# A chain of two transformer models: expert weights loaded in runs of 4 KB, two transfers a unit

## The reference

```
order = jnp.argsort(flat_e)                       # token-expert pairs sorted by expert
...
xs = x_pad[row_tok].reshape(n_blocks, MOE_BLOCK, D)          # blocks of 128 rows
def expert_block(args):
    xb, e = args
    return (jax.nn.silu(xb @ w_gate[e]) * (xb @ w_up[e])) @ w_down[e]
...
out = jnp.zeros((N + 1, D), ys.dtype).at[row_tok].add(ys)[:N]
```

## Time and profile before

| | us |
|---|---|
| median of 3 runs | 3743.65 (3742.29 to 3743.70) |
| span of the profiled execution, first to last instruction | 3737.3 |
| PE busy in it | 3342.8 (89%) |
| DVE busy | 1622.3 (43%) |
| transfers of queue q1 (hardware, which SP issues on) | 737.20 MB, 49.5% of 16 engines' time |

### The profile page before, as it was taken

How to read it: one execution, slowest core, us unless ns; L and a number is a source line. 1 busy time by engine, 2 the same in 40 slices (tenths; PEclk the granted TensorE clock), 3 DMA queues, 4 the chain that set the end, 5 groups by cost and what they waited for, 6 DMA issues and landing times. The chain is left out here.

```text
span 3737.3 us, 51196 instructions
## 1 busy us (share of the span) xinstructions
PE 3342.8 (89%) x20706; PEld 1722.0 (46%) x20706; DVE 1622.3 (43%) x2561; ACT 816.9 (22%) x1811; POOL 364.5 (10%) x355
## 2 busy tenths in 40 slices
PE   7999899699999698999995999995999968886996
PEld 3444565333333244777753333332555658443332
DVE  3660886511011574777755011113333874453114
ACT  0000660100000122555501000001333542010112
POOL 1000300210000000000001100000000900003110
PEclk9999999799999899999997999998999979887998
DMA  9990211599999622000024999997213200419996
GB/s 382 353 319 1 91 69 68 228 405 427 424 423 423 233 79 78 4 1 1 1 102 181 401 426 425 427 422 290 97 69 112 102 1 4 172 67 347 417 419 269
DMA packets 146708, 818.39 MB, mean 219 GB/s; under 512 B 29891, under 2 KB 35651, under 8 KB 100390
## 3 DMA queue, kind: packets, MB, share of 16 engines
q1 hardware_dynamic: 117494, 737.20, 49.5%
q0 software_dynamic: 25808, 68.88, 4.8%
q10 hardware_dynamic: 3168, 8.96, 0.6%
HBM read 752.52 MB, written 82.55 MB: 223 GB/s over the span
## 5 line engine op out<-in xcount | busy, mean ns | idle before, releaser
L2272 PE MATMUL m_yp<-m_w,m_hidT 128*32 128x512 f32 (+2 forms) x2248 | 377.2, 594 | 9.2 <-DVE m_yt L2025 3.8
L2249 PE MATMUL m_up<-m_w,m_xT 128*32 128x512 f32 (+2 forms) x1792 | 304.7, 606 | 21.1 <-DMA m_w<-in_moe_w_up 21.1
L2249 PE MATMUL m_gp<-m_w,m_xT 128*32 128x512 f32 (+2 forms) x1792 | 304.9, 600 | 9.4 <-DMA m_w<-in_moe_w_gate 5.9
L2030 DVE TENSOR_TENSOR m_hid<-m_sg,m_up 128x512 f32<-128x512 f32 x42 | 28.9, 687 | 578.4 <-PE m_up L2249 578.4
L2025 DVE TENSOR_TENSOR m_yt<-m_yp,keep_flat 128x512 f32<-128x512 f32 x128 | 82.4, 686 | 392.9 <-PE m_yp L2272 388.9
L412 PE MATMUL front_acc<-front_hT,front_wt 128*128 128x512 f32 x512 | 224.2, 599 | 7.2 <-DMA front_wt<-in_na_w_qkv 7.2
L2272 PEld LDWEIGHTS m_yp<-m_w,m_hidT 128*32 128x32 f32 (+2 forms) x2248 | 121.1, 123 | 217.0 <-issue 211.6
L2249 PEld LDWEIGHTS m_up<-m_w,m_xT 128*32 128x32 f32 (+2 forms) x1792 | 104.0, 126 | 216.1 <-issue 216.1
L2327 ACT ACTIVATE m_sg<-m_gp 128x512 f32<-128x512 f32 (+1 forms) x64 | 33.5, 524 | 772.9 <-PE m_gp L2249 543.7
L2249 PEld LDWEIGHTS m_gp<-m_w,m_xT 128*32 128x32 f32 (+2 forms) x1792 | 99.5, 125 | 209.0 <-issue 207.3
L1191 PE MATMUL n_acc<-n_wt,n_hT 128*128 128x512 f32 (+2 forms) x512 | 191.0, 529 | 2.5 <-DMA n_wt<-in_w_in 1.8
(11 more groups left out here) (493 smaller groups left out, 4936.3 us busy)
## 6 DMA issues: line engine op xcount, KB each, us to landing
m_w<-in_moe_w_gate SPq DMA_DIRECT2D x64, 2048.0 KB
m_w<-in_moe_w_up SPq DMA_DIRECT2D x64, 2048.0 KB
m_w<-in_moe_w_down SPq DMA_DIRECT2D x64, 2048.0 KB
v<-in_ada_w SPq DMA_DIRECT2D x40, 1024.0 KB, 12.7
m_w<-in_moe_w_gate SPq DMA_DIRECT2D x32, 1024.0 KB
m_w<-in_moe_w_up SPq DMA_DIRECT2D x32, 1024.0 KB
m_w<-in_moe_w_down SPq DMA_DIRECT2D x32, 1024.0 KB, 26.5
v<-in_w_mod SPq DMA_DIRECT2D x24, 1024.0 KB, 11.5
```

Source lines behind the costliest of these rows:

```text
L2249: last = pe.matmul(acc[part, 0:F], xT[:, j, k, part], w[:, place_of[m_, r][0], k * F:(k + 1) * F], start=k == 0, stop=k == KC - 1)
L2272: last = pe.matmul(yp[e][part, :], hidT[:, k, part], w[:, place_of["d", r][0], k * D + e * 512:k * D + (e + 1) * 512], start=k == 0, stop= ...
```

## The change

Each unit's one transfer becomes two. The new function `strips` views the partition's 16 KB (8 KB) as runs of 1024 numbers, 4 KB, and takes every second one: the first transfer has the runs 0 and 2, the second the runs 1 and 3 (in the third mixture run 0 and run 1). Slot and memory are viewed alike, so the data land where they did. No two runs of one transfer touch. Both transfers add 16 to the slot's semaphore, and PE waits for 32 a use. The loads of the spill loop stay as they are.

```diff
@@ -1895,6 +1895,10 @@
         def cols(e):
             return slice(e * 512, (e + 1) * 512)
 
+        def strips(v, odd):
+
+            return v.rearrange("p (a b n) -> p b a n", b=2, n=D)[:, odd]
+
         at = {}
         with st.block() as block:
 
@@ -2074,7 +2078,8 @@
                     expert = sp.value_load(pl[0:1, r:r + 1], min_val=0, max_val=LAYERS_EXPERTS - 1)
                     if before is not None:
                         sp.wait_ge(done[before[0]], before[1] + 1)
-                    sp.dma_start(w[:, slot], sources[m_][ds(expert, 1)].rearrange("a p n -> (a p) n")).then_inc(w_in[slot], 16)
+                    for odd in range(2):
+                        sp.dma_start(strips(w[:, slot], odd), strips(sources[m_][ds(expert, 1)].rearrange("a p n -> (a p) n"), odd)).then_inc(w_in[slot], 16)
 
                 for unit in layout.units[:AHEAD]:
                     load(*unit)
@@ -2224,7 +2229,7 @@
                 def arrived(m_, n):
                     for r, _, _ in layout.blocks[n][1]:
                         slot, use = place_of[m_, r]
-                        pe.wait_ge(w_in[slot], 16 * use)
+                        pe.wait_ge(w_in[slot], 32 * use)
 
                 def gate_up(n):
                     j = n % 2
```

## The result

The changed kernel takes 3805.55 us (median, 3802.5 to 3807.63) against 3743.68 us (3742.29 to 3746.32) for the kernel before in runs on the same chip: a ratio of 1.0163, 95% interval 1.0151 to 1.0175. It is slower, as forecast, but by 62 us and not by 25: above the range's upper end of 3793. The profiled execution spans 3800.4 us, 63.1 more than before.

A forecast was written before the change was run, and what follows sets the result against it. The weight transfers on full DMA engines were taken to bound mixtures 1 and 2, with the third nearly tied. 11.5 + 11.5 + 2.5 = 25.5 us on the span of 3737.3 gives 3762.8, plus 6.35 makes 3769; range 3750 to 3793.

The forecast's parts named there:

- The mixtures are bound by their transfers, and nothing else moves: Three mixtures: DMA share 1.01 mid-stage; transfers set the length of 1 and 2, nearly tie in 3; between them nothing moves.
- the engines are full from the first load: Mixtures 1 and 2: engines full from the first load (700) to the last, so all added transfer time lies on the path.
- Runs of 4 KB cost 0.12 us a unit more: Mixtures 1 and 2: 4 KB runs pass slower than 16 KB; 96 x 0.12 = 11.5 us a mixture (0 to 32).
- Mixture 3: +2.5: Third mixture: 4 KB in place of 8 KB runs costs 3.6 us over 96 units, the first covered, so 2.5.
- the cover that I had forecast: Third mixture's end: a unit lands at 3657.6, PE begins its block at 3658.68, so about 1 us of cover.
- A fixed tail: End of mixtures 1 and 2: length is the transfers' total service time plus a fixed tail; no growth priced.
- The full queue costs nothing: SP's issues: more packets hold SP up oftener and longer, but queued transfers feed the engines; priced at 0.
- Rival C: Queue runs dry on some engines, or runs with holes are read slower: 398 GB/s, +75 us, 3819; chance 0.09.
- My own sign for a wrong forecast: Forecast wrong if the share fell under 0.98 in a mixture's middle, or extra time stood at a mixture's start.
- Rival B: Mixtures' starts: shorter packets let q0's small transfers and instruction fetches through; about 10 us faster, 3734; chance 0.06.
- The rule of a fixed cost for each transfer: Skill page: about 2.0 us a transfer, 192 us a mixture if paid serially; taken as hidden, left out.
- the size of 1 MiB: Skill page's rule set against the change: it asks for at least 1 MiB a transfer.

## Why the prediction was wrong

The sign was right, and so was the mechanism of the largest part: more packets for the same bytes, in mixtures bound by their transfers. Its size was not, and two terms stood at nothing. Of the 37.6 us that the forecast lacks (63.1 less 25.5), 16.0 are the packets' rate in mixtures 1 and 2, 4.4 the packets in mixture 3, 15.8 the starts and 3.4 the ends, which were both put at nothing; -2.0 are elsewhere.

- *The mixtures are bound by their transfers, and nothing else moves.* Right: the share is over 1 in the middles, and the rest of the kernel changed by -2.0 us. But "the engines are full from the first load" overlooked the start: the share was full there, the bytes were not.
- *Runs of 4 KB cost 0.12 us a unit more.* The step that failed most. It is 0.209 and 0.197, within the bounds (0 to 0.335), 20.1 and 18.9 us a mixture in place of 11.5. The mistake was the row that I took it from: 413 GB/s from one stretch of 8 us with 835 packets, in which nothing else was queued, and then a value under what even that row gave (0.144). The kernel's middle moves 407, and the run with side-by-side rows shows 407 too, so it was not the holes that the row lacked. What made that stretch faster was not looked into. The rows of before held a hint to the right size: 425.1 and 419.1 GB/s for 16 and 8 KB are 4.93 and 5.00 us for 2.097 MB, 0.07 for 8 more packets on each engine; at that price 24 more cost 0.21.
- *Mixture 3: +2.5.* It is 9.8. By 9 ns a packet, 8 more on each engine for 96 units make 6.9 us, of which I had 3.6. Unit 95 lands 11.0 us later, so some 4.1 us are the start; PE's end is 1.2 us shorter, about the cover that I had forecast.
- *A fixed tail.* It grew by 2.3 us in each large mixture. I had priced PE's waits at their length alone; behind a longer one PE also runs its next group at the lower clock. In mixture 1 that makes 1.69 us of the 2.3 (8.78 against 7.09 us for the last up product; the windows of 1230 to 1250 have a clock of 0.95 and 0.88, against 1.00 in the earlier trace rows).
- *The full queue costs nothing.* Right in mixtures 1 and 2: an issue takes 2.2 us at the median and up to 6.0 us, unit 6 goes out 22 us late in mixture 1, and the run that brings it forward again wins nothing there. In mixture 3 it may cost 2 to 3 us.
- *Rival C, holes read slower.* I weighed it for the whole length and gave it 0.09. At the start something of the kind is seen, where it costs some 3 to 4 us in mixture 1, and not in the middle. My own sign for a wrong forecast, extra time at a mixture's start, is what came.
- *Rival B* has nothing for it: 700 to 800 us move less, and PE's wait for the first gathered rows in mixture 3 went from 10.5 to 9.3 us, without an effect.
- The rule of a fixed cost for each transfer, left out of the sum, was rightly left out: 192 further transfers in a mixture cost 3.4 us. Nor did the size of 1 MiB, which the prediction sets against the change, speak against all of it: in mixtures 1 and 2 the new transfers are still 1.049 MB each, which is 1 MiB, and only those of mixture 3 are smaller.

The corrected sum: 20.1 + 18.9 + 6.9 for the packets, 5.2 + 6.5 + 4.1 for the starts, 2.3 + 2.3 - 1.2 for the ends, -2.0 elsewhere: 63.1 us. The terms are parts of the measured whole, so that they add up proves nothing; that the packets' terms are one thing and the starts' another is what the experiments show. Mixture 3's 4.1 is what 9 ns a packet leaves over there; the run with strips in the head alone bears it out in part (3.5 us for 0.9). What the starts' 15.8 us are made of is known only in part, and only for mixture 1.

## What to carry to other kernels

Where the DMA engines are full, count packets, not transfers: each further packet cost about 9 ns on its engine here whatever its size, so keep each partition's run as long as it is (16 KB beat 8, 4 and 2 KB in this order). If a load must be cut into two transfers, cut it along the run (1% of this kernel with halves of 8 KB) and not by partitions (21%). Take a rate from a long stretch under the kernel's own load or from the difference between two long stretches, not from 8 us of another stage. And a low share or a slow engine that catches the eye in a new profile is a suspect only: take the suspect away and see whether the stage gets shorter. Here the share came back, and mixture 1 took as long as before.

## What the runs showed of the hardware

- About 9 ns for each packet on its engine from 16 KB down to 2 KB: 424, 418, 407 and 386 GB/s. The Trainium skill (page "DMA: Bandwidth & Descriptors", section "Why small descriptors are slow (HBM only)") tells of a fixed overhead of about 3 cycles a packet and draws its consequence for packets of 256 bytes. The direction agrees; here the overhead is worth 4% of the rate at 4 KB already.
- Transfers over 64 partitions moved 225 GB/s from 780 to 1180 us with all 16 engines busy, half of the 424 that 128 partitions get, and up to 358 later in the same mixture. So a full share doesn't tell the rate.
- SP's issue of a transfer of 256 packets in strips takes 0.54 us and more where one of 128 takes 0.33. Over all of mixture 1 the median is 2.2 us and the longest 5.9, with transfers queued all the time.
- Many of SP's branches and register instructions took 0.7 us each from about 724 to 743 us, while GpSimd issued the scatter of token numbers, and 0.03 to 0.05 us before and after it. What holds them wasn't tried.
